# Two of the three gate tiles of each differential-attention pass: logistic from an exponential and a reciprocal in place of the tangent

## The reference, cut to what matters

```python
def diff_blocks(q, k, v, lam):
    scale = q.shape[-1] ** -0.5
    def blk(qb):
        s = jnp.einsum('bqhsd,bkhsd->bhsqk', qb, k).astype(jnp.float32) * scale
        p = jax.nn.softmax(s, axis=-1)
        a = (p[:, :, 0] - lam * p[:, :, 1]).astype(v.dtype)
        return jnp.einsum('bhqk,bkhd->bqhd', a, v)
    return over_query_blocks(blk, q)
...
    o_diff = (rmsnorm(o_diff, lp['diff_subln']) * (1.0 - lam_init)).reshape(b, n, GROUP_W)
    o_hy = hyena(hy_in, lp)
    o = jnp.concatenate([o_mla * jax.nn.silu(m_gate), o_gqa * jax.nn.silu(g_gate),
                         o_diff * jax.nn.silu(d_gate), o_hy * jax.nn.silu(hy_gate)], axis=-1)
```

## Time and profile before

| | |
|---|---|
| median of 3 runs | 3079.74 us (3077.52 to 3082.14) |
| the profiled execution's own time | 3077.83 us |
| its span, first to last instruction | 3076.0 us |
| mean granted TensorE clock | 0.897 of full speed |
| PE busy | 2543.6 us, 83% |
| DVE busy | 1330.3 us, 43% |
| ACT busy | 941.1 us, 31% |
| POOL busy | 387.1 us, 13% |

### The profile page before, as it was taken

The page is one execution under the profiler, slowest core; times in us unless marked ns, Lnnn a source line. Parts: engine busy times, 40 slices in busy tenths (PEclk is TensorE's granted clock), DMA queues, the critical chain, the costliest instruction groups (busy, mean ns, idle before and its releaser), DMA issues. The chain is left out here.

```text
span 3076.0 us, 33678 instructions
## 1 busy us (share of the span) xinstructions
PE 2543.6 (83%) x13152; PEld 1653.7 (54%) x13152; DVE 1330.3 (43%) x2498; ACT 941.1 (31%) x1962; POOL 387.1 (13%) x280
## 2 busy tenths in 40 slices
PE   4969688888988987878959696798889889878798
PEld 1645555565456754654426455555654657556543
DVE  3242653443545354661133425534434544545611
ACT  1131102443244254461011320024421443544610
POOL 1220551000100000001213105510001000000012
PEclk9979889998999987888969798899989999878799
DMA  5420100100000000001143201001000000000021
GB/s 192 168 103 23 45 1 14 43 1 12 30 28 1 10 1 2 29 28 70 60 163 140 103 23 45 1 14 43 1 12 30 28 1 10 1 2 29 28 76 62
DMA packets 71848, 128.41 MB, mean 42 GB/s; under 512 B 22882, under 2 KB 35554, under 8 KB 70052
## 3 DMA queue, kind: packets, MB, share of 16 engines
q1 hardware_dynamic: 71688, 126.23, 11.9%
HBM read 109.02 MB, written 21.92 MB: 43 GB/s over the span
## 5 line engine op out<-in xcount | busy, mean ns | idle before, releaser
L588 PE MATMUL psum<-arena 128*32 128x256 f32 (+8 forms) x8496 | 1779.7, 456 | 232.4 <-POOL arena L1933 53.0
L588 PEld LDWEIGHTS psum<-arena 128*32 128x32 f32 (+3 forms) x8496 | 1033.1, 164 | 905.4 <-issue 627.6
L592 PE MATMUL psum<-ident,arena 128*128 128x128 f32 (+1 forms) x2248 | 415.1, 313 | 234.9 <-ACT arena L1241 143.0
L592 PEld LDWEIGHTS psum<-ident,arena 128*128 128x128 f32 (+1 forms) x2248 | 287.6, 155 | 388.5 <-ACT arena L1241 175.6
L1689 DVE TENSOR_REDUCE st<-psum 128x1 f32<-128x1152 f32 (+1 forms) x288 | 354.0, 1236 | 298.0 <-PE psum L588 297.4
L1425 DVE TENSOR_TENSOR arena<-arena 128x64 f32<-128x64 f32 (+9 forms) x638 | 328.9, 559 | 171.7 <-ACT arena L1376 61.4
L1241 ACT COPY arena<-psum 128x512 f32<-128x512 f32 (+1 forms) x472 | 206.7, 438 | 474.1 <-PE psum L592 473.4
L1225 ACT ACTIVATE arena<-psum,st 128x1152 f32<-128x1152 f32 (+1 forms) x288 | 325.6, 1131 | 79.8 <-DVE st L1689 70.9
L588 PE MATMUL psum<-k_parts,q_parts 96*128 96x384 f32 (+2 forms) x1000 | 297.3, 396 | 24.2 <-ACT arena L1225 13.5
L1933 POOL TENSOR_TENSOR arena<-arena 128x512 f32<-128x512 f32 (+2 forms) x98 | 273.3, 2804 | 294.5 <-DVE arena L1505 131.2
L1933 POOL TENSOR_TENSOR st<-st,mhalf 128x1 f32<-128x1 f32 (+2 forms) x72 | 56.3, 782 | 1555.9 <-DVE st L1430 1555.9
(11 more groups left out here) (126 smaller groups left out, 1247.0 us busy)
## 6 DMA issues: line engine op xcount, KB each, us to landing
arena<-in_ada_w SPq DMA_DIRECT2D x12, 2048.0 KB, 8.6
arena<-in_w_in SPq DMA_DIRECT2D x10, 2048.0 KB, 7.8
arena<-out_xs SPq DMA_DIRECT2D x36, 512.0 KB, 5.1
out_xs<-arena SPq DMA_DIRECT2D x18, 512.0 KB, 2.6
arena<-in_w_out SPq DMA_DIRECT2D x4, 2048.0 KB, 8.0
out_xs<-in_x SPq DMA_DIRECT2D x1, 4608.0 KB, 17.3
spectrum_kept<-arena SPq DMA_DIRECT2D x2, 2304.0 KB, 6.9
arena<-spectrum_kept SPq DMA_DIRECT2D x2, 2304.0 KB, 8.4
```

What stands on the lines that cost most here:

```text
L588: return nc.tensor.matmul(out, lhsT, rhs, start=start, stop=stop)
L592: return nc.tensor.transpose(out, src, ident[0:n, 0:n])
```

## The change

Parts 1 and 2 of each pass, those inside `attention`, get functions of their own. ScalarE takes exp(-x) with the table that is loaded anyway; VectorE adds 1 and clamps at 3e38, takes the reciprocal, and multiplies by 2 and by x, so that what is written is the same value as before. Part 0 and all other gates keep the tangent.

```diff
+                def gate_exp(f, i):
+
+                    job, n = ("gate", "diff", f, i), PARTS[i][1]
+                    act.wait_ge(*K.full(job))
+                    act.wait_ge(*K.emptied(("gate", "diff", f, i - 1)))
+                    nc.scalar.activation(at(TH["diff"], n), B(job, n), ACT.Exp, scale=-1.0
+                                         ).then_inc(*S.up("gate_exp", (f, i)))
...
                             f = int(grp[4])
-                            gate_tanh("diff", f, job[1], [(f, i) for i in range(3)])
-                            nc.scalar.preload_act_table_set("natural_log_exp_and_others")
+                            gate_exp(f, job[1])
...
+                def gate_quotient(f, i, dst):
+
+                    job, (tok, n), e = ("gate", "diff", f, i), PARTS[i], at(TH["diff"], PARTS[i][1])
+                    v.wait_ge(*S.at("gate_exp", (f, i)))
+                    link(nc.vector.tensor_scalar(e, e, 1.0, 3.0e38, ALU.add, ALU.min))
+                    link(nc.vector.reciprocal(e, e))
+                    nc.vector.scalar_tensor_tensor(at(dst + f * TOK + tok, n), e, 2.0, B(job, n), ALU.mult, ALU.mult
+                                                   ).then_inc(*K.drained(job))
...
                                 f = int(grp[4])
-                                gate_finish("diff", f, job[1], [(f, i) for i in range(3)], OT + 4 * TOK)
+                                gate_quotient(f, job[1], OT + 4 * TOK)
```

## The result

The changed kernel takes 3121.66 us (median of 4 runs, 3114.56 to 3124.63), the kernel before, timed beside it, 3079.05 (median of 4). The ratio is 1.0134, 95% interval 1.0115 to 1.0153: 1.3% or about 42 us slower. The forecast was 3101 us with a range of 3086 to 3111. The direction was right; the loss is twice what I gave it.

A forecast was written before the change was run, and what follows sets the result against it. It took a chain without slack (gate matmul, ScalarE, VectorE, bank 7 free, value matmuls) to bound step 9. VectorE's 16.2 us plus 4.8 us of lowered clock, 21.0 us, gave 3101 us, range 3086 to 3111.

The forecast's parts named there:

- The wait for bank 7 has no slack, and VectorE's two instructions come through whole: At step 9 TensorE already waits for VectorE's chain, so 3.02 us come through whole; at step 13 it moves 1.0 us.
- The loads are hidden: Sixteen table loads, 20.5 us of ScalarE's time at steps 9 and 13, were costed at nothing when removed.
- the reading of step 13 as two chains that end together: At step 13 ScalarE's and VectorE's chains end within 0.04 us of each other; the loads are on ScalarE's alone.
- The price of the reciprocal: On VectorE, 4.7 ns an element from rows of 1 and 4 elements: 2.5 us for 512, 0.75 for 128.
- The upper bound: Reciprocal at 6.5 ns an element, from a fixed part of 142 ns: 3.47 us for 512, 0.97 for 128.
- direct term: VectorE's added instructions at eight places, 3.02 us per 512 elements and 1.03 per 128, four of each: 16.2 us.
- Speaks for fewer: The 14 ns between two short reciprocal rows was taken to mean fewer than eight cycles an element on VectorE.
- The clock: Value matmuls after step 9 meet lowered clock, 1.2 us longer at four places, 4.8 us; nothing added at step 13.
- The sum: Over the whole kernel, 16.2 + 4.8 = 21.0 us slower, 3101 us for the median, 0.7% slower.
- the dear reciprocal: Rival: VectorE's reciprocal takes 4.49 and 1.22 us, places together 25.9 us, with the clock 3110 to 3112; chance 0.13.

The follow-up runs named there:

- bank 7 freed early: Changed kernel, but ScalarE first copies x from bank 7 to SBUF: 0.9997 of the kernel before; the kernel before with that copy, tangent and loads kept: 1.0031.
- loads-only run: Kernel before with the exponential and no table loads, VectorE's single gate instruction kept as (e + 1) times x: 3078.71 us, ratio 0.9993.
- quotient-only run: Kernel before with tangent and table loads kept, VectorE doing add, reciprocal and product: 3114.42 us, 1.0114 of the kernel before.
- cheap-instruction run: Changed kernel with the reciprocal replaced by a product with 0.5 of the same shape: 3094.14 us, 1.0043 of the kernel before.
- filled gaps: Light set of unread 128-column matmuls in differential attention steps: on the kernel before 3061.88 us (0.9937), with early release and exponential 3042.00 us (0.9874).

## Why the prediction was wrong

*The wait for bank 7 has no slack, and VectorE's two instructions come through whole*: right. 4.73 - 0.89 = 3.84 us at step 9 and 1.13 at step 13, four times each, are 19.9 us.

*The loads are hidden*: right (0.9993), and so was the reading of step 13 as two chains that end together. The runs with bank 7 freed early and with the added matmuls showed how near the second one lies: there the loads set the time.

*The price of the reciprocal*: inside its bounds, but the value taken was low, 2.5 and 0.75 us for 3.35 and 0.95. It came from a slope of 14 ns over three elements, where the wide tiles have 6.25 each; that a floor hides part of the slope in so short rows fits, but wasn't tested. The upper bound, 3.47 and 0.97, was nearly exact. This makes the direct term 19.9 us instead of 16.2. "Speaks for fewer" than eight cycles was right: by the estimate above it is six.

*The clock*: the step that failed. It read "in each of the four places at step 9 I expect them to meet a lowered stretch and take 1.2 us longer, 4.8 us in all", and "at step 13 they run at 0.77 already, and I add nothing". Measured is 42.6 us between the medians, less 19.9: about 23 us, nearly five times the term. In the profiled execution (36.8 us, so 16.9 beside the direct part) the value matmuls of step 10 take 6.13 to 6.40 us at the four places for 4.09 each, 8.7 us in all. Those of step 14 take 6.49 to 6.56 for 5.26, 4.09, 5.64 and 4.09, 7.0 us. I had read step 13 in the first layer's `diff0` alone, where the clock was already low; in two of four passes it was at full. From the value matmuls of step 6 to those of step 18 the four passes are 9.0, 13.1, 6.2 and 13.0 us longer, 41.4 in all, 21.5 beside the direct part; the 15.7 us of the value matmuls are most of that. What lies outside the passes gives 4.6 us back on balance. The first `diff0` starts 3.6 us late, ahead of any changed instruction, but so does that of the loads-only run, by 5.1, and the quotient-only run's starts 5.0 us early: that is scatter between executions. What puts the clock down at a given place stays open. In every unfilled kernel with a wait of 4.7 us at step 10 the value matmuls behind it take 5.6 to 7.0 us, but behind waits of 1.8 to 2.0 us in the cheap-instruction run they take 4.09 at some places and 5.8 to 6.9 at others.

*The sum* of 21.0 us thus had its direct term 3.7 us short and its clock term 18 us short, and the range's upper end came from the dear reciprocal with at most 1.6 us of clock at each of four places, which couldn't reach. No rival had a larger clock term. The forecast's sign and its mechanism for the wait stood; the failed step is the size of the clock term, 4.8 us at step 10 and nothing at step 14, for about 23 us measured in all.

## What to carry to other kernels

Ask of every microsecond that an engine gains where the other engine would wait for it: here 20.5 us off ScalarE were worth nothing, and 20 us more of wait for VectorE cost 42. If TensorE's wait grows in a kernel like this one, allow for lowered clock behind it as large as the wait itself, with a range down to nothing where the surroundings are kept busy, and read the clock at every place of the pattern, not at one. A second chain that ends within 0.04 us of the first is off the path only until the first one or TensorE gets faster. Before making a function cheaper, look at what holds the PSUM bank: one copy out of it took the slow work off the path. The filled gaps paid without it too, but half as much as beside it.

## What the runs showed that I had not expected

The fp32 reciprocal on VectorE takes 3352 ns for 128 x 512 and 953 ns for 128 x 128, 6.25 ns an element, while an add with a clamp takes 426 and 219. Three matmuls of 128 columns a step that nobody reads made the kernel before 0.6% faster, and the one with the early release and the exponential 1.3%, with TensorE's mean granted clock at 0.920 and 0.923 instead of 0.897 and 0.895, though they add work to the engine that is busiest.
